# The sample's attention moved into the prompt attention's pipeline, one layer step on one core of Trainium2

## What is computed

```python
def stick_breaking_block(q, k, v, q_pos, k_pos):
    """A[t,s] = sigmoid(z_ts) * prod_{s<j<t} (1 - sigmoid(z_tj)), s < t."""
    z = einsum('bhtd,bhsd->bhts', q, k) * (SB_DIM ** -0.5)
    mask = k_pos[None, :] < q_pos[:, None]
    log_beta = where(mask, log_sigmoid(z), -inf)
    log_1m = where(mask, log_sigmoid(-z), 0.0)
    rest = cumsum(log_1m, axis=3, reverse=True) - log_1m
    a = exp(log_beta + rest)
    return einsum('bhts,bhsd->bhtd', a, v)
```

## Time and profile before

| | |
|---|---|
| time before, median of 3 runs | 3626.03 us (3625.22 to 3630.92) |
| the profiled execution: its time / its span | 3625.41 / 3623.8 us |
| PE busy | 3289.2 us (91%) |
| DVE busy | 1609.5 us (44%) |
| ACT busy | 1058.6 us (29%) |
| POOL busy | 784.8 us (22%) |
| granted TensorE clock, mean | 0.934 of full |

### The profile page before, as it was taken

The page is one execution under the profiler, slowest core; times in us unless marked ns, Lnnn a source line. Parts: engine busy times, 40 slices in busy tenths (PEclk is TensorE's granted clock), DMA queues, the critical chain, the costliest instruction groups (busy, mean ns, idle before and its releaser), DMA issues. The chain is left out here.

```text
span 3623.8 us, 47465 instructions
## 1 busy us (share of the span) xinstructions
PE 3289.2 (91%) x17583; PEld 2886.8 (80%) x17583; DVE 1609.5 (44%) x2098; ACT 1058.6 (29%) x2037; POOL 784.8 (22%) x669
## 2 busy tenths in 40 slices
PE   6699999996999994988698599999999997799999
PEld 2488887775999994767586599999999997687786
DVE  4200000554889896663454544444444443422422
ACT  4211111223777773213322522222222111311210
POOL 2311010332666663001100411111111110200200
PEclk7799999998999997995799699999999998899999
DMA  5122111446224220652343211111111111533532
GB/s 181 50 73 70 67 67 50 137 128 160 52 51 91 49 51 28 214 174 84 120 159 123 88 47 47 47 47 47 47 47 47 47 47 49 184 134 130 178 134 70
DMA packets 242097, 327.25 MB, mean 90 GB/s; under 512 B 57356, under 2 KB 164292, under 8 KB 234772
## 3 DMA queue, kind: packets, MB, share of 16 engines
q1 hardware_dynamic: 229678, 285.39, 25.7%
q0 software_dynamic: 12000, 40.18, 3.3%
q10 hardware_dynamic: 292, 0.02, 0.0%
HBM read 225.56 MB, written 99.98 MB: 90 GB/s over the span
## 5 line engine op out<-in xcount | busy, mean ns | idle before, releaser
L1791 PE MATMUL facc<-h2H,fwH 128*128 128x416 f32 x1760 | 617.5, 351 | 17.8 <-POOL fwL L1727 17.8
L1791 PE MATMUL facc<-h2L,fwH 128*128 128x416 f32 x1760 | 617.3, 351 | 0.0
L1791 PE MATMUL facc<-h2H,fwL 128*128 128x416 f32 x1760 | 617.2, 351 | 0.0
L519 PE MATMUL pacc<-pwH,h1H 128*128 (+1 forms) x952 | 379.3, 398 | 27.7 <-POOL pwL L446 22.1
L519 PE MATMUL pacc<-pwH,h1L 128*128 (+1 forms) x952 | 373.9, 393 | 0.0
L519 PE MATMUL pacc<-pwL,h1H 128*128 (+1 forms) x952 | 373.8, 393 | 0.0
L743 POOL TENSOR_TENSOR aS<-aS,aC 128x512 f32<-128x512 f32 (+3 forms) x320 | 332.9, 1046 | 186.1 <-DVE aC L714 173.9
L1750 DVE TENSOR_SCALAR fV<-fU,fcw,fcb 128x2048 f32<-128x2048 f32 x88 | 112.3, 1318 | 579.2 <-ACT fU L1696 579.2
L714 DVE TENSOR_TENSOR_SCAN aC<-aB,aC,a 128x512 f32<-128x512 f32 (+3 forms) x320 | 356.6, 1114 | 24.8 <-ACT aB L690 18.9
L1791 PEld LDWEIGHTS facc<-h2H,fwH 128*128 128x128 f32 x1760 | 331.0, 188 | 20.7 <-ACT fwH L1684 18.2
L1694 ACT ACTIVATE fU<-facc 128x416 f32<-128x416 f32 (+1 forms) x220 | 113.1, 514 | 801.3 <-PE facc L1791 801.3
(11 more groups left out here) (270 smaller groups left out, 5106.9 us busy)
## 6 DMA issues: line engine op xcount, KB each, us to landing
da<-act_d SPq DMA_DIRECT2D x32, 1408.0 KB, 7.1
proj_out<-pstage SPq DMA_DIRECT2D x119, 256.0 KB, 2.0
fraw<-w_up SPq DMA_DIRECT2D x44, 512.0 KB
act_d<-fV SPq DMA_DIRECT2D x22, 1024.0 KB, 5.3
aq<-qk_T SPq DMA_DIRECT2D x32, 512.0 KB
mwa<-w_ada SPq DMA_DIRECT2D x16, 1024.0 KB, 5.5
praw<-w_in SPq DMA_DIRECT2D x56, 256.0 KB
mx<-proj_out SPq DMA_DIRECT2D x51, 256.0 KB
```

The lines of the kernel that those rows point to most:

```text
L519: mm = nc.tensor.matmul(acc[:, t % NB].unsqueeze(1), a[:, kk, t * P:(t + 1) * P], w[:, at[kk], :], start=(kk == 0 and n == 0), stop=(kk == ...
L1791: mm = nc.tensor.matmul(dst, a[:, j, kk], h[:, kk, cols], start=(kk == 0 and m == 0), stop=(kk == KD - 1 and m == 2))
```

## The change

- The stage `attention_sample` is deleted, with its triangular sums, its splitting into high and low parts and its fold.
- `attention` works off a list of 336 items in place of 320 chunks. Ten items are set into head 1's forty, at every fifth place: one that turns the sample's queries (QUERIES) and nine that turn a block of keys each (KEYS, 4 transposes each, all in fp32). Six items are put ahead of head 3's (SAMPLE): two rows, each with four heads of 32 queries in its 128 partitions, over 9 blocks of keys in three chunks of 128, 512 and 512 columns.
- A SAMPLE chunk's scores are two products in plain fp32 (qs and ks) instead of fp32r; its product with V has 256 columns (four heads' values) instead of 64.
- In a step PE now does `turn`, `z`, `av` in that order.
- SP loads the sample's keys, values and queries after it has stored row 8 of head 0. Q, K, V of head 4 are loaded after the SAMPLE rows' stores. POOL sets three small tiles at the start of the stage.
- `w_out` is loaded in `mlstm`, after the last chunk's loads and ahead of the wait for the last modulation row, and SP waits for it there.

```diff
+    PROMPT, SAMPLE, KEYS, QUERIES = range(4)
+    heads = [[(PROMPT, h, i, g) for i in range(NPT) for g in reversed(range(i // W4 + 1))] for h in range(SH)]
+    aside = [(QUERIES, 0, 0, 0)] + [(KEYS, b, 0, 0) for b in range(NPB1)]
+    for n, item in enumerate(aside):
+        heads[1].insert(5 * n + 2, item)
+    heads[3] = [(SAMPLE, half, NPB, g) for half in range(2) for g in reversed(range(NPB // W4 + 1))] + heads[3]
+    items = [item for head in heads for item in head]
...
+            def load_sample():
+                own = tok(NPT)
+                sp.dma_start(xq[:], d["proj_out"][5, own, :]).then_inc(past_k_in, 16)
+                for x, g, cache, sem in ((xk, 6, "past_k", past_k_in), (vs, 3, "past_v", past_v_in)):
+                    sp.dma_start(x[:, 0:NPB], d[cache].rearrange("(b p) n -> p b n", p=P)).then_inc(sem, 16)
+                    sp.dma_start(x[:, NPB], d["proj_out"][g, own, :]).then_inc(sem, 16)
...
+            load(1)
+            for m in last_of:
+                kind, h, i, g = items[scored[m]]
+                if kind == PROMPT and i == 0 and 0 < h < SH - 1:
                     load(h + 1)
+                store(scored[m])
+                if kind == PROMPT and (h, i) == (0, NPT // 2):
+                    load_sample()
...
         def take(eng, copy, n):
             eng.wait_ge(turned, n + 1)
-            at_least(eng, av_done, n - RA + 1)
-            copy(part(A, RA, n), part(X, NX, n)).then_inc(taken[n % 2], 1)
+            kind, a, i, g = items[n]
+            if kind == KEYS:
+                op = copy(ks[:, :, a * P:(a + 1) * P], X[:, n % NX].rearrange("p (j t) -> p j t", t=P))
+            elif kind == QUERIES:
...
+            else:
+                at_least(eng, av_done, rank[n] - RA + 1)
+                op = copy(part(A, RA, n), X[:, n % NX, 0:width(n)])
+            op.then_inc(taken[n % 2], 1)
...
+                else:
+                    for u in range(2):
+                        pe.wait_ge(taken[u], ...)
+                    at_least(pe, stop_ready, m - NZ + 1)
+                    for j in range(2):
+                        mm = nc.tensor.matmul(to, qs[:, 2 * h + j], ks[:, 2 * h + j, span], start=(j == 0), stop=(j == 1),
+                                              skip_group_check=True)
...
+                    value = V[:, h % 2, b] if kind == PROMPT else vs[:, b, h * 4 * SD:(h + 1) * 4 * SD]
+                    mm = nc.tensor.matmul(O[:, r % 2, 0:SD if kind == PROMPT else 4 * SD], weight[:, j * P:(j + 1) * P], value,
...
             for n in steps:
-                on(z, n + 4)
-                on(turn, n - 3)
-                on(av, n - 6)
-
-
-def attention_sample(k, c, w_out):
...
+                every(turn, n - 3)
+                scores(z, n + 4)
+                scores(av, n - 6)
...
             tiles(sp, body)
+            sp.dma_start(w_out[:], d["w_out"].rearrange("(k p) n -> p k n", p=P)).then_inc(w_out_in, 16)
+            sp.wait_ge(w_out_in, 16)
             sp.wait_ge(mod_row, NPT)
...
-            attention_sample(k, c, w_out)
-            k.end_phase()
```

More of the change, by code:

```diff
@@ L624, in row, with top, last, prompt_row @@
         def row(n):
-            h, i, g = chunks[n]
-            return h * NPT + i
[L629 to L636, removed]
+            return row_of[rank[n]]
+        def top(n):
+            return rank[n] in tops
+        def last(n):
+            return rank[n] in last_of
+        def prompt_row(n):
+            kind, h, i, g = items[n]
+            return h * NPT + i
         def part(ring, depth, n):
-            return ring[:, n % depth, 0:width(n)]
+            return ring[:, rank[n] % depth, 0:width(n)]
         def left(n):
-            h, i, g = chunks[n]
+            kind, a, i, g = items[n]
             at = SEQ - (i + 1) * P + W4 * g * P
             return C[:, row(n) % RC], at, at + width(n)
-        def on(op, n):
+        def scores(op, n):
+            if n in rank:
+                op(n, rank[n])
+        def every(op, n):
             if 0 <= n < N:
@@ new lines, in store @@
+            def store(n):
+                kind, h, i, g = items[n]
+                r = row(n)
+                sp.wait_ge(o_taken, r + 1)
+                if kind == PROMPT:
+                    p = prompt_row(n) % RO
+                    sp.dma_start(d["o_d"][tok(i), h * SD:(h + 1) * SD], of[:, p]).then_inc(stored[p], 16)
+                else:
+                    for j in range(4):
+                        at = (4 * h + j) * SD
+                        sp.dma_start(d["o_d"][SEQ:SEQ + DEC, at:at + SD],
+                                     ofs[j * DEC:(j + 1) * DEC, h, j * SD:(j + 1) * SD]).then_inc(sample_stored, 16)
@@ L699, in _ @@
             for n in steps:
-                on(passing, n + 2)
-                on(stopping, n + 2)
-                on(take_even, n - 4)
+                scores(passing, n + 2)
+                scores(stopping, n + 2)
+                every(take_even, n - 4)
         @block.vector
@@ L719, in take_odd, with out @@
                     take(dve, v.tensor_copy, n)
[L721 to L726, removed]
+            def out(n, m):
+                if not last(n):
+                    return
+                dve.wait_ge(av_done, m + 1)
+                kind, h, i, g = items[n]
+                if kind == PROMPT:
+                    p = prompt_row(n)
+                    at_least(dve, stored[p % RO], 16 * (p // RO))
+                    v.tensor_copy(of[:, p % RO], O[:, row(n) % 2, 0:SD]).then_inc(o_taken, 1)
+                else:
+                    v.tensor_copy(ofs[:, h], O[:, row(n) % 2, 0:4 * SD]).then_inc(o_taken, 1)
             v.memset(nought[:], 0.0).then_inc(nought_set, 1)
@@ L730, in _ @@
             for n in steps:
-                on(passed, n)
-                on(take_odd, n - 4)
-                on(out, n - 7)
+                scores(passed, n)
+                every(take_odd, n - 4)
+                scores(out, n - 7)
         @block.gpsimd
@@ L762, in turn, with av @@
             def turn(n):
[L763 removed]
+                kind, a, i, g = items[n]
+                if kind in (KEYS, QUERIES):
+                    pe.wait_ge(past_k_in, 48)
+                    src, parts = (xk[:, a] if kind == KEYS else xq), 4
+                else:
+                    pe.wait_ge(w_ready, rank[n] + 1)
+                    src, parts = part(S, RS, n), len(blocks(n))
                 if n >= NX:
                     pe.wait_ge(taken[n % 2], n // 2)
[L766 to L768 removed]
+                for j in range(parts):
+                    mm = nc.tensor.transpose(X[:, n % NX, j * P:(j + 1) * P], src[:, j * P:(j + 1) * P], c["ident"][:])
                 mm.then_inc(turned, 1)
[L771 to L772 removed]
+            def av(n, m):
+                kind, h, i, g = items[n]
                 r = row(n)
@@ L1131, in _, with mlstm @@
                              start=True, stop=True).then_inc(dec_sum, 1)
-def mlstm(k, c, gc, dec):
+def mlstm(k, c, gc, dec, w_out):
     nc, d = k.nc, k.d
```

329 lines of the change are left out of this document (79 added, 250 removed).

## The result

The changed kernel takes 3527.61 us (median of 4 runs, 3525.11 to 3528.02) against 3625.62 us for the kernel before (4 runs, 3622.08 to 3630.92): a ratio of 0.9725, 95% interval 0.9713 to 0.9738, 98 us less. The forecast was 3529.0 us. The profiled execution took 3528.02 us with a span of 3526.4.

What follows compares the result with a forecast made beforehand. PE was taken to bound the attention and latency the sample's stage. 3625.4 - 120.4 (stage) + 23.0 (PE work added in the attention) + 0.5 (buffer waits) + 0.5 (w_out) = 3529.0 us; forecast 3522 to 3536 (0.68), range 3514 to 3546.

Steps and rivals of the forecast that it cites:

- What bounds the kernel, and what goes: PE limits the attention, latency the sample's stage; deleting that stage removes its whole 120.4 us, none hidden under another stage.
- The turned blocks: In the attention, 58 added turns on PE at 0.12 us each cost 7.0 us (6.4 to 8.1).
- The plain fp32 scores: In the attention, the two sample rows' scores cost PE 7.8 us, at 0.432 us per 256-column product, scaled by columns.
- The rival of cheap products: Plain fp32 products take 0.24 us for 512 columns, so scores and V products shrink to about 4 us: 3517; chance 0.06.
- The products with V: In the attention, the sample's 18 blocks of 256 columns at 0.432 us each cost PE 7.8 us.
- DVE, ACT, POOL at nothing: Work added on these engines in the attention, about 10 us on DVE, hides under PE's time and costs nothing.
- The two X buffers at the set-in items: In head 1, turns waiting for copies out of two buffers cost 0 to 4 us, taken as 0.5.
- The rival that made 12 us of them: Bubbles: each of nine places in the attention costs a scan's length, 1.3 us, 12 us in all: 3540; chance 0.13.
- The order turn, z, av at nothing: PE's new order in an attention step costs nothing, since the same work lies between like instructions.
- w_out in mlstm: The load moved into mlstm ends near 1611, 5 us before SP needs it; 0.5 us added (0 to 3).
- Later stages at nothing: Stages after the change are untouched and cost nothing, though a shift of TensorE's clock may move a few us.
- The slower case: The new order makes the attention bound by its chain; to lose, over 97 us, 0.30 us every step; chance 0.02.

Runs made afterwards that it cites:

- before_w_out_early: The kernel before with w_out's load moved into mlstm as in the change and the sample's own stage kept: ratio 0.9998 to before.
- after_z_first: The changed kernel with PE's order in a step put back to z, turn, av: 3530.66 us, 0.9731 of before.

## Why the prediction was right, and where it was wrong

*What bounds the kernel, and what goes.* Right. 120.4 us went, the seam behind mlstm has its old length, and neither the load of w_out nor anything else had shared in the stage (before_w_out_early).

*The turned blocks.* Right: 0.122 us each against 0.12.

*The plain fp32 scores.* Right in mechanism and price: 0.43 us for an instruction of 512 columns. The rival of cheap products falls, and with it, by these rows, the reading by which the gap in the Trainium skill's TensorE page ("TensorE: Matmul & The Clock Gate", "Back-to-back issue gap") holds for every type.

*The products with V.* The same row's price holds here too. Eight instructions of 256 columns in the changed kernel, on the weight loads, start at 1095.20 and the next turns at 1096.94:

```profile
1095.20 1.71 PEld L872 LDWEIGHTS a_out<-bv,aA 128*128 128x128 f32 x8
1096.94 0.57 PEld L856 LDWEIGHTS a_x<-ident,aS 128*128 128x128 f32 x4
```

1.74 us for eight, 0.218 each against 0.216. For the six items as a whole I had 18.1 us and the runs say 18.3 to 18.6.

*DVE, ACT, POOL at nothing.* Right: DVE had half of the time to spare in the sample rows.

*The two X buffers at the set-in items.* I took 0.5 us; the run without the sample's rows leaves 0.1 to 0.4. after_z_first, with the order whose step length the forecast took, leaves no room for bubbles either: all items together cost 22.0 us there, less than the 23.5 with the 0.5 in it. Which of its terms was too dear by 1.5 us under that order no run parts. The rival that made 12 us of them falls.

*The order turn, z, av at nothing.* This is the step that failed. I argued that between like instructions the same work stands, and took from it that the step's length is the same. But a step's length is also what each instruction costs behind its neighbour. The earlier trace rows had shown it: I wrote myself that the turns' 0.56 us "holds the tail of the second z product" and did not ask whether another neighbour would carry a shorter one. It is worth 4.7 us by itself and 3.3 in the changed kernel. With it the attention grows by 4.9 + 18.3 - 4.7 = 18.5 us. That sum is put together from differences between runs, so it has to meet the 18.1 to 19.4 us of the traces with this attention; what checks the forecast are its terms, 4.8 and 0.5 against 4.9, 18.1 against 18.3, and nothing against 4.7. By the other way round the items cost 22.0 us with the old order and the order takes 3.3 off again.

*w_out in mlstm.* Right: it landed 15.5 us after its issue, 3.7 us before the last modulation row. I had expected 5 us of slack. SP's wait there, to be read beside the earlier trace rows:

```profile
SPq L1086 <- DVE mmod_rows L1193: 18.7, 1, 18.7
```

The view counts the load's landing into that wait, since the row came last.

*Later stages at nothing.* Wrong by 4 us, 3.1 of them in ffn_down. I had named a shift of the clock as the risk, and it is half of the 3.1 us; but the unchanged kernel has it in one of two traces, so it needs no change of the program. The other half is a longer idle time of PE that I did not see coming and can't explain.

The nearness of the total is thus in good part luck: -4 us in the attention against +4 us behind it. With the terms as measured, and nothing for the later stages, the same sum gives 3625.4 - 120.4 + 18.5 + 0.1 = 3523.6.

*The slower case.* The chain did not take over: PE's waits for copies are few and 0.8 us at the longest. What the new order took from the slack is visible (12 waits of PE for DVE's copies in the changed kernel, 5.4 us in all), but it is small against the 97 us from which it would have decided.

The changed kernel with fp32r scores is the fastest that was run, 3519.5 us, at the price of the low bits named above.

## What to carry to other kernels

Where stages are parted by barriers, a stage bound by a chain of short dependent steps costs its whole length, and its work may cost a fifth of that (here 22 of 120 us, in another form and without the high and low parts) as further items in a pipeline that keeps one engine full; price it on that engine alone, then look for the engine with the least slack. When the full engine's instructions change places, don't reason from the waits alone: take the length of each group behind its neighbour from the timeline, since a step can be shorter or longer by a few per cent with the same instructions. And before an effect in one part of a pipeline is believed, sum over the part behind it: a change of places moved 1.7 us from one head to the next, and nothing else. In the same way, take a second trace of the unchanged kernel before you explain a few us in a stage that nobody touched.

## What the runs showed of the hardware

A step of 14 PE instructions took 1.80 us with turns behind a product of 512 columns and 1.75 us with products of 64 columns behind it, in all 79 such steps of either kernel. In plain fp32 an instruction of 512 columns took 0.43 us and one of 256 columns 0.22, with the clock granted in full; each product is two of them. 3.4 us at the lower clock level, 1.2 GHz, cost a stretch of PE work of 248 us 1.6 us. A stage of some 550 us that the change did not touch had PE idle for 1.8 to 2.2 us at one place in five traces and for 3.0 to 4.4 us in seven others, parted by whether the program held the old stage's code and not by when the stage ran.
